# First FFN of a two-block kernel: x laid out by features as a second input, the norm's factor put on gate sums and residual, first units loaded by halves

## Chip, cores and metric

One core of a Trainium2 chip runs the whole program in one launch. The metric is the device time in microseconds of one execution; three executions of the kernel before took 1588.74, 1589.74 and 1584.87 us, median 1588.74.

## The reference, cut to what matters

A sequence of 256 tokens with 1024 features passes two blocks in fp32: FFN, attention mixer, FFN, norm; then, twice, FFN, mixer (RWKV, then stick-breaking attention), FFN with layer norms. The change concerns the very first sublayer:

```
def rmsnorm(x, g):
    xf = x.astype(jnp.float32)
    y = xf * lax.rsqrt(jnp.mean(xf * xf, axis=-1, keepdims=True) + RMS_EPS)
    return (y * g.astype(jnp.float32)).astype(x.dtype)

def swiglu(h, w_gate, w_up, w_down):
    return (jax.nn.silu(h @ w_gate) * (h @ w_up)) @ w_down

x = x + 0.5 * swiglu(rmsnorm(x, norm_ffn1[l]), w_ffn1_gate[l], w_ffn1_up[l], w_ffn1_down[l])
```

The FFN's hidden width is 2816, 22 tiles of 128. The factor 1/sqrt(mean) is one number per token, so it can be put on the products as well as on x.

## The kernel before

**Units.** All weights come as "units" of 128 x 2048 fp32 (1024 KB) in the order of use, from `ws`. The first FFN has 33 units: a gate unit holds one 128-column tile of the gate matrix (s = 0) and one of the up matrix (s = 1), a down unit holds two 128-row tiles of the down matrix. The order (`ffn_order`, L53) is gate 0, gate 1, then nine times (gate 2j+2, down j, gate 2j+3), then gate 20, gate 21, down 9, down 10. So unit 3 is the first "down".

**Split.** Each value is a sum of a high part (rounded to the format fp32r) and a low part (the rest). ScalarE writes the high part of a unit (`hi_to`, L200, instruction at L210), VectorE subtracts it for the low part (`lo_to`, L213, instruction at L224). There are three raw buffers, four high and three low ones. SP loads unit u (`load_units`, L186) once the low part of unit u-3 has been written, since then its raw buffer is free. A product is high x high, high x low and low x high. TensorE reads x as `xt`: features on the partitions, eight blocks of 128 features, two halves of the tokens, high and low.

**Beginning (L3128 to L3159).** SP loads x by two halves of tokens (512 KB each), the gain row broadcast to all partitions (512 KB), units 0 to 2, small vectors, constants. ScalarE squares x with a row sum (L348) and takes the root (L350), VectorE the mean and reciprocal, and multiplies x by the token's factor and by the gain row (L336). TensorE turns the result by sixteen transposes (L247), ScalarE and VectorE copy it from PSUM as high and low parts (L277, L284). Then TensorE multiplies units 0, 1 and 2: first high x (high, low) of the first tokens (`first_tensor`), then the rest (`second_tensor`). Their sums go into banks 0 to 5.

**FFN.** From unit 3 each engine has its own program. For unit n ScalarE (`ffn_scalar`, L693) first makes high parts up to unit n+3, waiting for its load, and only then treats gate n: it copies the cross products of the gate tile from PSUM (`lead_scalar`, L488, for the first three units; `wide_scalar`, L609, for the others), silu of the gate sum (L707, with a table load ahead of the first), the cross products of the up tile, and the high part of the hidden tile (L716). VectorE (`ffn_vector`, L724) first makes low parts up to unit n+2, then adds cross products and own products (L501 for the first three, L616 for the others) for s = 0 and s = 1, multiplies silu and up sum (L742) and subtracts the high part (L745). Each of these orders is fixed, and a wait holds whatever stands behind it.

TensorE (`ffn_tensor`, L644) waits for the low part of the unit. A gate unit takes eight matmuls of 512 columns and eight of 256 for each s. From unit 4 they go into three banks in turn (`gate_bank`, L574), and a bank is taken again when the event `s_tt` of the sum that read it has come:

```
    banks = (6, 4, 5) if t == "f1" else (6, 7, 4, 5)
    q = 2 * (f - 3) + s
```

So the up tile of gate f waits for the gate sum of gate f-1, and the gate tile of f for the up sum of f-2. The first down unit waits for the up sum of gate 1 as well.

**Beside it.** After gate 3 TensorE makes a small product of distances into bank 7 (`bias_tensor`, L1112). VectorE copies it, and POOL writes it out eight times, 512 KB each (`bias_pool`, L1139), the i-th behind the product of silu and up of gate 2+i; two large reads follow. These writes share the DMA engines with the units.

Of the kernel before, what the change touches and what calls it, by code (L numbers as in the profile page):

```python
# [8 lines left out]
F32 = mybir.dt.float32  # L9
# [105 lines left out]
def tiles_and_signals(nc, ctx, k):  # L115
# [5 lines left out]
    def sig(name):  # L121
# [187 lines left out]
class Rms:  # L309


    def __init__(self, k, t, scale, sums, ready, gain, free=None):

        self.k, self.t, self.scale, self.sums, self.ready, self.gain, self.free = k, t, scale, sums, ready, gain, free

    def add_vector(self, dve, a, h):
        k = self.k
        if self.sums is None:
            return
        dve.wait_ge(*self.sums(a, h))  # L320
        xs = k.x[:, a, h * 512:(h + 1) * 512]
        dve.e.scalar_tensor_tensor(out=xs, in0=k.P[2 * a + h][:, :], scalar=self.scale, in1=xs, op0=ALU.mult,
                                   op1=ALU.add).then_inc(*k.s_res.inc(self.t, a, h))

    def rest_vector(self, dve, a):
# [12 lines left out]

    def scalar(self, act, a):
        k, t = self.k, self.t  # L340
        if self.sums is None:
            act.wait_ge(*self.ready(a))
        else:
            for h in range(2):
                act.wait_ge(*k.s_res.after(t, a, h))
# [267 lines left out]
def wide_vector(k, dve, event, b, cross, out, scale=1.0):  # L613

    dve.wait_ge(*k.s_tb.after(*event))
    dve.e.scalar_tensor_tensor(out=out.rearrange("p (a t) -> p a t", a=2), in0=wide_parts(k, b)[0], scalar=scale,  # L616
                               in1=cross.rearrange("p (a t) -> p a t", a=2), op0=ALU.mult,
                               op1=ALU.add).then_inc(*k.s_tt.inc(*event))


def down_tensor(k, pe, u, j, i, a, hs=(0, 1)):
# [319 lines left out]
def mixer_tiles(k):  # L941
# [37 lines left out]
    k.MV = ar(k, 20480, 512, "p (a c) -> p a c", a=2)  # L979
    k.MEM = ar(k, 3072, 2048, "p (a n) -> p a n", a=2)  # L980
    k.JUNK = k.XN
    k.cross, k.mx_cross = crosses(k, 15360), crosses(k, 15856)


# [126 lines left out]

def bias_tensor(k, pe, j):  # L1112
    if j == 0:
        pe.wait_ge(*k.s_base.after())
        pe.wait_ge(*k.s_rel.after())
        mm(pe, k.P[7][0:16, :], k.RELX, k.BASE).then_inc(*k.s_pe.inc("dist"))
# [1926 lines left out]


def sync_program(k, sp):
    for a in range(2):
        sp.e.dma_start(k.x[:, a, :], k.x_in[a * 128:(a + 1) * 128, :]).then_inc(*k.s_x[a].inc(by=16))
    load_gains(k, sp, "f1", (0,))
    load_units(k, sp, 0, NRAW)
    sp.e.dma_start(k.vc[:, :], k.vec[:, :]).then_inc(*k.s_vec.inc(by=16))  # L3050
    sp.e.dma_start(k.cs[:, C_TRI:C_END], k.cst[:, C_TRI:C_END]).then_inc(*k.s_cst.inc(by=16))

    def gains(name, rows_, after):
        for w in after:
# [10 lines left out]
    gains("f2", (2,), normed("mx"))  # L3065
    load_units(k, sp, U_MIX + 10, U_FFN2 + 6)
    gains("f3", (3,), normed("f2"))
    load_units(k, sp, U_FFN2 + 6, U_FFN3 + 6)
    gains("rw", (4, 5), normed("f3"))
    load_units(k, sp, U_FFN3 + 6, U_RWKV + 15)  # L3070
    gains("f4", (6, 7), [k.s_pe.after("read", 1)])
# [3 lines left out]
    gains("f5", (8, 9), normed("f4"))  # L3075
    load_units(k, sp, U_FFN4 + 6, U_FFN5 + 6)
    gains("sb", (10, 11), normed("f5"))
    load_units(k, sp, U_FFN5 + 6, U_FFN6 + 1)
    gains("f6", (12, 13), [k.s_tr.after("sbmemo")])
    load_units(k, sp, U_FFN6 + 1, U_FFN6 + 6)  # L3080
    gains("end", (14, 15), normed("f6"))
    load_units(k, sp, U_FFN6 + 6, NU)
    for a in range(2):
        for h in range(2):
            sp.wait_ge(*k.s_xn.after("end", a, h))
        sp.e.dma_start(k.out[a * 128:(a + 1) * 128, :], k.x[:, a, :]).then_inc(*k.s_out.inc(a, by=16))
    sp.wait_ge(*k.s_out.after(1))


def pool_program(k, pool):  # L3090
    pool.e.dma_start(k.cs[:, 0:C_TRI], k.cst[:, 0:C_TRI]).then_inc(*k.s_id.inc(by=16))
    pool.e.dma_start(k.BASE, k.base[:, :]).then_inc(*k.s_base.inc(by=16))
    pool.e.dma_start(k.RELX, k.relx[:, :]).then_inc(*k.s_rel.inc(by=16))
    bias_pool(k, pool)
# [17 lines left out]
def norms(k):  # L3112

    k.norm = {
        "f1": Rms(k, "f1", 1.0, None, lambda a: k.s_x[a].after(), "f1"),
        "mx": Rms(k, "mx", 0.5, ffn_sums(k, "f1", U_FFN1), None, "mx", "f1"),
        "f2": Rms(k, "f2", 1.0, rows_done(k, "mx", U_MIX + 19), None, "f2", "mx"),
        "f3": Rms(k, "f3", 0.5, ffn_sums(k, "f2", U_FFN2), None, "f3", "f2"),
        "rw": LayerNorm(k, "rw", 0.5, ffn_sums(k, "f3", U_FFN3), "rw"),
        "f4": LayerNorm(k, "f4", 1.0, rows_done(k, "rw", U_RWKV + 14), "f4"),  # L3120
        "f5": LayerNorm(k, "f5", 0.5, ffn_sums(k, "f4", U_FFN4), "f5"),
        "sb": LayerNorm(k, "sb", 0.5, ffn_sums(k, "f5", U_FFN5), "sb"),
        "f6": LayerNorm(k, "f6", 1.0, rows_done(k, "sb", U_SB + 13), "f6"),
        "end": LayerNorm(k, "end", 0.5, ffn_sums(k, "f6", U_FFN6), "end"),
    }


def begin_tensor(k, pe):  # L3128

    turn_tensor(k, pe, "f1", tiles(k.XN), halves(k.s_xn, "f1"))  # L3130
    units = first_units(U_FFN1)
    for n in range(3):
        first_tensor(k, pe, "f1", units[n], n)
    for n in range(3):
        second_tensor(k, pe, "f1", units[n], n)


def begin_scalar(k, act):
    act.wait_ge(*k.s_dv.after("one"))
    act.e.activation(k.sm[:, 31:32], k.sm[:, 30:31], ACT.Sqrt)  # L3140
    for a in range(2):
        k.norm["f1"].scalar(act, a)
    turn_scalar(k, act, "f1", None, FIRST, (4, 5))
    hi_to(k, act, U_FFN1 + 1)
    turn_scalar(k, act, "f1", None, SECOND, (6, 7))
    hi_to(k, act, U_FFN1 + 3)


def begin_vector(k, dve):
    dve.e.memset(k.sm[:, 30:31], 1.0).then_inc(*k.s_dv.inc("one"))  # L3150
    for a in range(2):
        k.norm["f1"].rest_vector(dve, a)
    turn_vector(k, dve, "f1", FIRST, (4, 5))
    lo_to(k, dve, U_FFN1)
    turn_vector(k, dve, "f1", SECOND, (6, 7))
    lo_to(k, dve, U_FFN1 + 2)


# [91 lines left out]
    vector_program(k, Stream(engines[4], real))  # L3250


def build(nc, ws, cst, vec, base, relx, gains, x_in, mem_in, lora, gup, w2, out):
    k = Space()
    k.ws, k.cst, k.vec, k.base, k.relx, k.gains, k.x_in, k.mem_in = ws, cst, vec, base, relx, gains, x_in, mem_in
    k.lora, k.gup, k.w2, k.out = lora, gup, w2, out
    with ExitStack() as ctx:
        tiles_and_signals(nc, ctx, k)
# [54 lines left out]
def lay_out(i):  # L3313
# [79 lines left out]
    for l in range(2):  # L3393
        for n in range(3):
            g2 += [i["ln_g_2"][l, n], i["ln_b_2"][l, n]]
    gains = np.stack([i["norm_ffn1"][0], i["norm_mix"][0], i["norm_ffn2"][0], i["norm_final"]] + g2)
# [22 lines left out]
```

## Time and profile before

| what | value |
|---|---|
| median of three runs | 1588.74 us (1584.87 to 1589.74) |
| span of the profiled execution | 1585.7 us (the page gives no other time of it) |
| TensorE busy | 1553.6 us, 98% |
| VectorE busy | 1037.7 us, 65% |
| ScalarE busy | 864.8 us, 55% |
| DMA | 285.08 MB, mean 180 GB/s |

All times on a row of the trace are microseconds from the first instruction of the span, so they stand a little under the device time of a run. "Busy" of TensorE counts pipelined matmuls, whose ends are modelled: the difference of two starts says more than a duration. A timeline row that merges n instructions gives the start of the first and the time to the end of the last.

### The profile page before, as it was taken

How to read it: one execution, taken by the hardware profiler on the slowest of the kernel's cores; microseconds unless marked ns; L12 is line 12 of the kernel's file. 1: busy time of each engine (PE TensorE's matmuls, PEld its weight loads, DVE VectorE, ACT ScalarE, POOL GpSimd, SP SyncE). 2: the span in 40 equal slices, each digit the busy share in tenths (PEclk: the TensorE clock that was granted, in tenths of full speed). 3: DMA queues.
4: the chain of work that ended last, by engine and by line, in shares of the span. 5: the costliest groups of instructions: out<-in, count | busy, mean ns of one | idle time of the engine just before them, and what ended most of it. 6: DMA issues, size and time to landing. Idle time of an engine off the chain costs nothing. (4 is left out here: it accounts for less than half of the span.)

```text
span 1585.7 us, 26471 instructions
## 1 busy us (share of the span) xinstructions
PE 1553.6 (98%) x11174; PEld 1355.8 (86%) x11174; DVE 1037.7 (65%) x1477; ACT 864.8 (55%) x1270; POOL 131.2 (8%) x124
## 2 busy tenths in 40 slices
PE   7999999999999999999999999999999999999998
PEld 6888888688888988889988888889888888898886
DVE  6556676766566665667965775657756675676566
ACT  6455556655555555556753365555655565665553
POOL 0000020000000010002564001000100010001000
PEclk9999999999999999999999999999999999999999
DMA  7997546246555465555310365553655542455551
GB/s 289 236 263 266 199 160 249 81 175 217 205 186 186 159 216 209 176 194 181 128 48 4 134 231 194 186 196 137 251 194 179 190 181 80 160 211 188 201 175 75
DMA packets 42133, 285.08 MB, mean 180 GB/s; under 512 B 4906, under 2 KB 4922, under 8 KB 10144
## 3 DMA queue, kind: packets, MB, share of 16 engines
q1 hardware_dynamic: 39024, 272.42, 48.8%
q0 software_dynamic: 2992, 10.99, 3.3%
q8 instruction: 88, 1.44, 0.4%
q14 instruction: 29, 0.24, 0.0%
HBM read 277.62 MB, written 5.24 MB: 178 GB/s over the span
## 5 line engine op out<-in xcount | busy, mean ns | idle before, releaser
L236 PE MATMUL P<-xt,whi 128*128 128x512 f32 (+1 forms) x3264 | 723.6, 345 | 6.4 <-DVE AR L616 2.3
L236 PEld LDWEIGHTS P<-xt,whi 128*128 128x128 f32 x3264 | 557.3, 190 | 76.6 <-issue 7.3
L224 DVE TENSOR_TENSOR wlo<-raw,whi 128x2048 fp32r<-128x2048 f32 x245 | 559.5, 2290 | 55.6 <-PE P L236 47.4
L210 ACT ACTIVATE whi<-raw 128x2048 fp32r<-128x2048 f32 x245 | 467.7, 1910 | 149.5 <-PE P L236 83.9
L236 PE MATMUL P<-xt,wlo 128*128 128x256 f32 x2544 | 439.7, 282 | 0.0
L236 PEld LDWEIGHTS P<-xt,wlo 128*128 128x128 f32 x2544 | 386.8, 191 | 17.8
L616 DVE SCALAR_TENSOR_TENSOR AR<-P,AR 128x256 f32<-128x256 f32 x228 | 96.2, 422 | 244.4 <-ACT AR L609 244.3
L236 PE MATMUL P<-whi,hh 128*128 128x512 f32 x504 | 197.4, 392 | 0.0
L236 PE MATMUL P<-wlo,hh 128*128 128x512 f32 x504 | 196.8, 391 | 0.0
L236 PE MATMUL P<-whi,hl 128*128 128x512 f32 x504 | 196.1, 389 | 0.0
L609 ACT ACTIVATE AR<-P 128x256 f32<-128x256 f32 x228 | 85.5, 375 | 118.0 <-PE P L236 117.9
L236 PE MATMUL P<-whi,xt 128*128 128x512 f32 (+2 forms) x400 | 125.5, 376 | 0.4 <-DVE xt L2645 0.4
L716 ACT ACTIVATE hh<-AR 128x256 fp32r<-128x256 f32 x126 | 52.7, 418 | 112.6 <-DVE AR L742 112.6
L236 PEld LDWEIGHTS P<-whi,hl 128*128 128x128 f32 x504 | 94.6, 188 | 20.2
L236 PEld LDWEIGHTS P<-whi,hh 128*128 128x128 f32 x504 | 94.8, 188 | 18.0
L236 PEld LDWEIGHTS P<-wlo,hh 128*128 128x128 f32 x504 | 94.9, 188 | 17.3
L707 ACT ACTIVATE AR<-AR 128x256 f32<-128x256 f32 x132 | 55.1, 418 | 91.0 <-DVE AR L616 84.7
L236 PE MATMUL P<-AR 64*64 64x64 f32 (+8 forms) x2422 | 95.8, 244 | 2.1 <-issue 1.1
L745 DVE TENSOR_TENSOR hl<-AR,hh 128x256 fp32r<-128x256 f32 x126 | 55.6, 441 | 61.0 <-ACT hh L716 61.0
L236 PEld LDWEIGHTS P<-AR 64*64 64x64 f32 (+6 forms) x2422 | 74.3, 139 | 19.6 <-issue 8.9
L236 PEld LDWEIGHTS P<-whi,xt 128*128 128x128 f32 x400 | 72.8, 189 | 13.4 <-issue 1.0
L515 POOL TENSOR_SCALAR x<-x 128x1024 f32<-128x1024 f32 x10 | 32.8, 3297 | 571.2 <-DVE AR L742 414.0
(228 smaller groups left out, 1012.6 us busy)
## 6 DMA issues: line engine op xcount, KB each, us to landing
raw<-ws SPq DMA_DIRECT2D x249, 1024.0 KB, 4.9
gb<-gains SPq DMA_DIRECT2D x14, 512.0 KB, 7.3
by_distance<-AR POOLq DMA_DIRECT2D x8, 512.0 KB, 8.3
AR<-by_distance POOLq DMA_DIRECT2D x1, 2048.0 KB, 17.1
AR<-by_distance POOLq DMA_DIRECT2D x1, 1536.0 KB, 9.1
x<-x_in SPq DMA_DIRECT2D x2, 512.0 KB, 3.8
AR<-mem_in POOLq DMA_DIRECT2D x1, 1024.0 KB, 5.2
AR<-gains SPq DMA_DIRECT2D x2, 512.0 KB, 4.6
```

Of the source, the lines that this page charges most:

```text
L210: act.e.activation(k.whi[n % NHI][:, :], k.raw[u % NRAW][:, :], ACT.Copy).then_inc(*k.s_hi.inc(u))
L224: dve.e.tensor_tensor(k.wlo[n % NLO][:, :], k.raw[u % NRAW][:, :], k.whi[n % NHI][:, :].bitcast(F32), ALU.subtract).then_inc(*k.s_lo.inc(u))
L236: return pe.e.matmul(o, l, r, start=start, stop=stop, skip_group_check=True)
L515: pool.e.tensor_scalar(k.x[:, a, :], k.x[:, a, :], ALPHA / scale, None, ALU.mult).then_inc(*k.s_al.inc(t, a))
L609: act.e.activation(cross.rearrange("p (a t) -> p a t", a=2), wide_parts(k, b)[1], ACT.Copy, scale=scale).then_inc(*k.s_tb.inc(*event))
L616: dve.e.scalar_tensor_tensor(out=out.rearrange("p (a t) -> p a t", a=2), in0=wide_parts(k, b)[0], scalar=scale, in1=cross.rearrange("p (a ...
L707: act.e.activation(k.SL[:, f % 2, :], k.cross[f % 3][:, 0, :], ACT.Silu).then_inc(*k.s_sl.inc(t, f))
L716: act.e.activation(hh, k.HF[:, f % 2, :].rearrange("p (a t) -> p a t", a=2), ACT.Copy).then_inc(*k.s_hh.inc(t, f))
L745: dve.e.tensor_tensor(hl, k.HF[:, f % 2, :].rearrange("p (a t) -> p a t", a=2), hh.bitcast(F32), ALU.subtract).then_inc(*k.s_hl.inc(t, f))
```

## The change

x comes a second time, laid out by features (`x_col`, 128 x 2056, made beside the other inputs): eight columns with the norm weights of the first FFN, then eight blocks of 128 features by 256 tokens. `xt` is made from it directly: ScalarE copies a block times its column of norm weights (high part), VectorE multiplies again and subtracts (low part). There is no turn. Units 0 and 1 are loaded, and their parts made, by halves (s = 0, s = 1), the first half's high part by quarters. TensorE takes all three units as it takes later ones: 512 columns of high by (high, low), then 256 of low by high, and waits per feature block at the beginning.

x by tokens is loaded behind and is still squared with a row sum; root and reciprocal give the token's factor. Two diagonal matrices with these factors, multiplied from the left by ones, put the factors as a row on all partitions (bank 7), and ScalarE copies it as `RROW`. VectorE multiplies every gate sum of the first FFN by `RROW` (22 times 128x256, ahead of silu), and the event for which ScalarE and the next user of the bank wait, `s_tt`, moves behind that multiplication. The up sums are not multiplied. The factor for them, times 0.5, is put on the residual (the scale of that addition is a column of factors instead of the constant 0.5). The gain rows lose their first row, and the mixer's gain row is loaded without a wait.

The core of the diff (changes of signatures and row numbers left out):

```diff
@@ lead_vector
-                                   op1=ALU.add).then_inc(*k.s_tt.inc(t, n, s))
+                                   op1=ALU.add).then_inc(*summed(k, t, n, s))
+        if rooted(t, s):
+            rooted_vector(k, dve, t, n, out[:, s, :])
+
+def rooted(t, s):
+    return t == "f1" and s == 0
+
+def summed(k, t, f, s):
+    return k.s_dv.inc("gate sum", f) if rooted(t, s) else k.s_tt.inc(t, f, s)
+
+def rooted_vector(k, dve, t, f, part):
+    dve.wait_ge(*k.s_ea.after("rrow"))
+    dve.wait_ge(*k.s_dv.after("gate sum", f))
+    dve.e.tensor_tensor(part, part, k.RROW, ALU.mult).then_inc(*k.s_tt.inc(t, f, 0))
@@ wide_vector: the same for the other gates
@@ sync_program
-    for a in range(2):
+    def tokens(a):
         sp.e.dma_start(k.x[:, a, :], k.x_in[a * 128:(a + 1) * 128, :]).then_inc(*k.s_x[a].inc(by=16))
-    load_gains(k, sp, "f1", (0,))
-    load_units(k, sp, 0, NRAW)
+    def part(u, s):
+        w = slice(1024 * s, 1024 * s + 1024)
+        sp.e.dma_start(k.raw[u][:, w], k.ws[u, :, w]).then_inc(*k.s_part[u][s].inc(by=16))
+    sp.e.dma_start(k.XCOL[:, 0:1032], k.x_col[:, 0:1032]).then_inc(*k.s_col[0].inc(by=16))
+    part(0, 0)
+    sp.e.dma_start(k.XCOL[:, 1032:2056], k.x_col[:, 1032:2056]).then_inc(*k.s_col[1].inc(by=16))
+    part(0, 1)
+    tokens(0)
+    part(1, 0)
+    tokens(1)
+    part(1, 1)
+    load_units(k, sp, 2, NRAW)
...
-    gains("mx", (1,), normed("f1"))
+    gains("mx", (0,), [])
@@ pool_program
+    pool.e.memset(k.ONE, 1.0).then_inc(*k.s_po.inc("one"))
@@ norms
-        "mx": Rms(k, "mx", 0.5, ffn_sums(k, "f1", U_FFN1), None, "mx", "f1"),
+        "mx": Rms(k, "mx", lambda a: k.sm[:, 12 + a:13 + a], ffn_sums(k, "f1", U_FFN1), "mx"),
+def begin_high_tensor(k, pe, u, s):
+    wh, _ = weights(k, u)
+    for c in range(8):
+        pe.wait_ge(*k.s_xl.after("f1", c))
+        if u == 2:
+            pe.wait_ge(*k.s_hi.after(u))
+        else:
+            pe.wait_ge(*k.s_hi.after("part", u, s, 1 if u or s else c // 4))
+        w = slice((s * 8 + c) * 128, (s * 8 + c) * 128 + 128)
+        mm(pe, k.P[LEAD_BANKS[u][s]][:, :], wh[:, w], k.xt[:, c, :, :, :].rearrange("p a s t -> p (a s t)"), c == 0, False)
@@ begin_tensor
+    for u in range(3):
+        for s in range(2):
+            begin_high_tensor(k, pe, u, s)
+        if u == 1:
+            pe.wait_ge(*k.s_po.after("one"))
+            for a in range(2):
+                pe.wait_ge(*k.s_dv.after("diag", a))
+                last = mm(pe, k.P[7][:, 128 * a:128 * a + 128], k.ONE, k.DIAG[:, a, :])
+            last.then_inc(*k.s_pe.inc("rrow"))
+        for s in range(2):
+            last = begin_low_tensor(k, pe, u, s)
+        last.then_inc(*k.s_used.inc(u))
@@ begin_scalar
+    for c in range(4):
+        high(c)
+    part(0, 0, 0, 1)
+    for c in range(4, 8):
+        high(c)
+    part(0, 0, 1, 2)
+    part(0, 1, 0, 2)
+    square(0)
+    part(1, 0, 0, 2)
+    square(1)
+    part(1, 1, 0, 2)
+    act.wait_ge(*k.s_var.after("f1"))
+    act.e.activation(k.sm[:, 6:8], k.sm[:, 10:12], ACT.Sqrt).then_inc(*k.s_rt.inc("f1"))
+    hi_to(k, act, U_FFN1 + 2)
+    act.wait_ge(*k.s_pe.after("rrow"))
+    act.e.activation(k.RROW, k.P[7][:, 0:256], ACT.Copy).then_inc(*k.s_ea.inc("rrow"))
     hi_to(k, act, U_FFN1 + 3)
```

VectorE's beginning follows the same order: eight low parts of x, low(0, 0), low(0, 1), low(1, 0), the mean, low(1, 1), the reciprocal, two diagonals (128x128), the half factor, the low part of unit 2.

## Rows read from the trace of the kernel before

**Rows 1.** The page's busy times by engine: us, share of the span, instructions.
```profile
PE 1553.6 (98%) x11174; PEld 1355.8 (86%) x11174; DVE 1037.7 (65%) x1477; ACT 864.8 (55%) x1270; POOL 131.2 (8%) x124
```

**Rows 2.** TensorE's waits, whole run: us in total, times, longest.
```profile
PE P L236 <- DVE AR L616: 2.3, 2, 1.2
```

**Rows 3.** TensorE's timeline, 8 to 116 us: start, us, instruction, [idle before <- releaser].
```profile
8.86 3.82 PE L247 MATMUL P<-cs,AR 128*128 128x128 f32 x16 [8.86 <-DVE AR L336]
13.28 4.10 PE L236 MATMUL P<-xt,whi 128*128 128x256 f32 x32 [0.61 <-ACT whi L210]
...
31.39 0.40 PE L236 MATMUL P<-whi,hh 128*128 128x512 f32 x1
...
36.86 1.98 PE L236 MATMUL P<-xt,whi 128*128 128x512 f32 x8
...
64.18 2.11 PE L236 MATMUL P<-xt,whi 128*128 128x512 f32 x8 [1.05 <-DVE AR L616]
...
82.29 2.11 PE L236 MATMUL P<-xt,whi 128*128 128x512 f32 x8 [1.23 <-DVE AR L616]
...
99.01 2.00 PE L236 MATMUL P<-xt,whi 128*128 128x512 f32 x8
```

**Rows 4.** ScalarE's timeline, 20 to 25 us.
```profile
20.58 1.92 ACT L210 ACTIVATE whi<-raw 128x2048 fp32r<-128x2048 f32 x1 [2.78 <-DMA raw<-ws]
23.91 0.66 ACT L493 ACTIVATE AR<-P 128x256 f32<-128x256 f32 x2 [1.41 <-PE P L236]
24.58 1.28 ACT L707 ACT_TABLE_LOAD   x1
```

**Rows 5.** VectorE's timeline, 7 to 30 us.
```profile
7.96 1.42 DVE L336 SCALAR_TENSOR_TENSOR AR<-x,sm,gb 128x512 f32<-128x512 f32 x2 [2.03 <-DMA gb<-gains]
...
27.65 2.28 DVE L224 TENSOR_TENSOR wlo<-raw,whi 128x2048 fp32r<-128x2048 f32 x1
29.85 0.74 DVE L501 SCALAR_TENSOR_TENSOR AR<-P,AR 128x256 f32<-128x256 f32 x2
```

**Rows 6.** SP's timeline, then DMA issues: times, KB each, us to landing.
```profile
0.73 0.84 SPq L3047 DMA_DIRECT2D x<-x_in  x2
4.13 0.44 SPq L3051 DMA_DIRECT2D cs<-cst  x1
...
x<-x_in SPq DMA_DIRECT2D x1, 512.0 KB, 3.4
x<-x_in SPq DMA_DIRECT2D x1, 512.0 KB, 4.2
cs<-cst SPq DMA_DIRECT2D x1, 752.0 KB, 13.3
raw<-ws SPq DMA_DIRECT2D x1, 1024.0 KB, 4.9
raw<-ws SPq DMA_DIRECT2D x1, 1024.0 KB, 13.8
```

**Rows 7.** Transposes: weight loads near 9 us, products near 200 us.
```profile
8.83 1.57 PEld L247 LDWEIGHTS P<-cs,AR 128*128 128x128 f32 x8 [8.83 <-issue]
...
200.00 0.60 PE L247 MATMUL P<-cs,AR 128*128 128x128 f32 x4
```

**Rows 8.** Stretches: us, PE, (PEld, DVE, ACT, POOL) busy, PEclk, DMA share, GB/s.
```profile
9.00:11.00 2.00, 2.00 (x10) 1.00 1.01 422
...
80.00:120.00 40.00, 38.77 (x208) 33.41 (x207) 23.81 (x27) 20.83 (x28) 2.87 (x4) 1.00 0.92 266
```

**Rows 9.** Waits for the raw buffers' loads, 0 to 140 us: us, times.
```profile
  DMA raw<-ws: 32.4, 10
```

**Rows 10.** ScalarE's timeline near 61 us.
```profile
61.49 1.92 ACT L210 ACTIVATE whi<-raw 128x2048 fp32r<-128x2048 f32 x1 [8.57 <-DMA raw<-ws]
```

**Rows 11.** VectorE's timeline: gate sums near 63 and 98 us.
```profile
63.70 0.42 DVE L616 SCALAR_TENSOR_TENSOR AR<-P,AR 128x256 f32<-128x256 f32 x1 [6.53 <-ACT AR L609]
...
98.37 0.42 DVE L616 SCALAR_TENSOR_TENSOR AR<-P,AR 128x256 f32<-128x256 f32 x1 [4.09 <-ACT AR L609]
```

More of the change, by code:

```diff
@@ L145, in tiles_and_signals @@
     k.s_gn = [sig("gn0"), sig("gn1")]
+    k.s_col = [sig("col0"), sig("col1")]
+    k.s_part = [[sig(f"part{u}{s}") for s in range(2)] for u in range(2)]
     k.s_id, k.s_vec, k.s_cst, k.s_base, k.s_rel = (
@@ L340, in scalar @@
         k, t = self.k, self.t
[L341 to L345, printed above, removed]
+        for h in range(2):
+            act.wait_ge(*k.s_res.after(t, a, h))
         if self.free is not None:
@@ L617, in wide_vector @@
                                in1=cross.rearrange("p (a t) -> p a t", a=2), op0=ALU.mult,
-                               op1=ALU.add).then_inc(*k.s_tt.inc(*event))
+                               op1=ALU.add).then_inc(*summed(k, *event))
+    if rooted(event[0], event[2]):
+        rooted_vector(k, dve, event[0], event[1], out)
 def down_tensor(k, pe, u, j, i, a, hs=(0, 1)):
@@ L1113, in bias_tensor @@
     if j == 0:
+        pe.wait_ge(*k.s_ea.after("rrow"))
         pe.wait_ge(*k.s_base.after())
@@ L3125, in norms, with begin_low_tensor @@
     }
-def begin_tensor(k, pe):
[L3130 to L3135, printed above, removed]
+def begin_high_tensor(k, pe, u, s):
[8 more added lines that the diff above has]
+        mm(pe, k.P[LEAD_BANKS[u][s]][:, :], wh[:, w], k.xt[:, c, :, :, :].rearrange("p a s t -> p (a s t)"), c == 0, False)
+def begin_low_tensor(k, pe, u, s):
+    _, wl = weights(k, u)
+    own, _ = lead_parts(k, u, s)
+    pe.wait_ge(*(k.s_lo.after(u) if u == 2 or s else k.s_lo.after("part", u)))
+    for c in range(8):
+        w = slice((s * 8 + c) * 128, (s * 8 + c) * 128 + 128)
+        last = mm(pe, own, wl[:, w], k.xt[:, c, :, 0, :], False, c == 7)
+    return last
+def begin_tensor(k, pe):
+    for u in range(3):
[10 more added lines that the diff above has]
+        last.then_inc(*k.s_used.inc(u))
 def begin_scalar(k, act):
@@ L3150, in begin_vector, with low @@
     dve.e.memset(k.sm[:, 30:31], 1.0).then_inc(*k.s_dv.inc("one"))
-    for a in range(2):
[L3152 to L3155, printed above, removed]
+    def low(u, s):
+        w = slice(1024 * s, 1024 * s + 1024)
+        dve.wait_ge(*k.s_hi.after("part", u, s, 1))
+        dve.e.tensor_tensor(k.wlo[u][:, w], k.raw[u][:, w], k.whi[u][:, w].bitcast(F32),
+                            ALU.subtract).then_inc(*(k.s_lo.inc(u) if s else k.s_lo.inc("part", u)))
+    for c in range(8):
+        dve.wait_ge(*k.s_xh.after("f1", c))
+        dve.e.scalar_tensor_tensor(out=k.xt[:, c, :, 1, :], in0=k.XRAW[:, c, :, :], scalar=k.GCOL[:, c:c + 1],
+                                   in1=k.xt[:, c, :, 0, :].bitcast(F32), op0=ALU.mult,
+                                   op1=ALU.subtract).then_inc(*k.s_xl.inc("f1", c))
+    low(0, 0)
+    low(0, 1)
+    low(1, 0)
+    for a in range(2):
+        dve.wait_ge(*k.s_sq.after("f1", a))
+    dve.e.tensor_scalar(k.sm[:, 10:12], k.sm[:, 4:6], 1.0 / DM, 1e-6, ALU.mult, ALU.add).then_inc(*k.s_var.inc("f1"))
+    low(1, 1)
+    dve.wait_ge(*k.s_rt.after("f1"))
+    dve.e.reciprocal(k.sm[:, 10:12], k.sm[:, 6:8]).then_inc(*k.s_dv.inc("f1", "rstd"))
+    dve.wait_ge(*k.s_id.after())
+    dve.wait_ge(*k.s_dv.after("f1", "rstd"))
+    for a in range(2):
+        dve.e.tensor_scalar(k.DIAG[:, a, :], k.cs[:, C_ID:C_ID + 128], k.sm[:, 10 + a:11 + a], None,
+                            ALU.mult).then_inc(*k.s_dv.inc("diag", a))
+    dve.e.tensor_scalar(k.sm[:, 12:14], k.sm[:, 10:12], 0.5, None, ALU.mult).then_inc(*k.s_dv.inc("f1", "half"))
+    dve.lo = U_FFN1 + 2
     lo_to(k, dve, U_FFN1 + 2)
@@ L3402, in lay_out @@
         "ws": ws, "cst": cst, "vec": vec, "base": base, "relx": relx, "gains": gains, "x_in": i["x"][0],
+        "x_col": np.concatenate([cols_of(i["norm_ffn1"][0]), by_cols(i["x"][0].T, slice(0, NT))], axis=1),
         "mem_in": i["mem_2"][0], "lora": lora, "gup": i["rwkv_g_up_2"][0],
```

57 lines of the change are left out of this document (33 added, 24 removed).

## Prediction

> **What bounds the kernel now.** I read the page's busy times first: TensorE is busy 98% of the span, VectorE 65%, so time can come only from TensorE's gaps or its work [rows 1]. Then TensorE's waits: in the whole run it waits twice for a gate sum, 2.3 us together [rows 2]. Its timeline shows both in the first FFN (they end at 64.18 and 82.29), and the beginning: nothing until the transposes at 8.86, the first matmul at 13.28, and from 17.86 no gap until the first "down" product at 31.39 [rows 3]. The change can take at most what lies ahead of 31.39. The timelines of ScalarE and VectorE tell who would hold TensorE if it came earlier, and the DMA issues when the data is there.
>
> **Until the first three units are multiplied.** What goes: the norm of x (square, root, reciprocal, product with the gain row, whose load VectorE awaits until 7.96), sixteen transposes (3.82 us) and their copies. What comes, for each of eight feature blocks: one ScalarE copy and one VectorE operation of 128x256. A pair of such copies takes ScalarE 0.66 us, so 0.33 each in a row; VectorE's pair takes 0.74 [rows 4, 5]. Loads land in the order of issue. The first 512 KB land at 0.73+3.4 = 4.1, the second, issued about 0.42 later, at 5.35 (4.2 behind it): 1.25 us per 512 KB. The gain row behind them took until 7.96, so 2.6 [rows 5, 6]. The new order (columns, half unit, columns, half unit, tokens, half, tokens, half, unit 2, vectors, constants) has two loads of 512 KB more, the columns, and lacks the slow gain row: two at 1.25 for one at 2.6. So the queue empties as before, at 4.13+13.3 = 17.4.
>
> Step by step: first columns 4.1; four copies to 5.5; first half unit 5.4. Second columns between 6.6 (by 1.25) and 7.96 (the gain row's place); I take 7.3, since POOL's small constants pass then too. Four copies to 8.6; the second quarter of unit 0's high part (a whole one takes 1.92, so 0.55 with its overhead) to 9.2; the next half (1.0) to 10.2. TensorE starts in earnest at 9.2 and is paced to 10.2. Then come 40 matmuls of 512 columns and 48 of 256. Eight of the first take 1.98 with a tail of 0.4, so 0.227 apart; 32 of the second 4.10, so 0.12 apart [rows 3]: 9.1+5.8, and 0.5 for the two products that make the row of factors, 15.4 in all. TensorE is through with three units at 25.6, not 31.39: 5.8 us earlier. Squares (1024 elements at ScalarE's rate: 1.0 each), root, reciprocal and two diagonals lie between, on engines that wait for loads, and TensorE has six blocks of work before it needs the factors.
>
> One cost is hidden here. The removed transposes ran 0.21 us apart (eight weight loads in 1.57 with a tail), the same operation at 200 us 0.11 (four in 0.60 with a tail of 0.27), though the granted clock is printed 1.00 from 9 to 11 us [rows 7, 8]. If the first sixteen wide matmuls run at half the rate instead, TensorE is through at 25.6+16x0.2 = 28.8. The Trainium skill, "TensorE: Matmul & The Clock Gate", section "What's actually happening", says that throttled is the default and that activity releases it. By it the transposes paid for the matmuls behind them, and the change hands the bill to the matmuls. The spacing agrees, the clock column doesn't; the next step makes either end harmless.
>
> **The first "down" product, where the gain is cut.** ScalarE's order has the high part of unit 3 ahead of the sums of unit 0. In the trace it waits 2.78 us for its load, starts at 20.58, and ScalarE still waits 1.41 for TensorE afterwards [rows 4]. Now TensorE is early and the load is last. Unit 3 is issued once unit 0's buffer is free, near 11, behind a queue that empties at 17.4; with 2.5 for its 1024 KB it lands at 20.0 (bounds: 19.0, and 25.4 if each half of a unit goes as the gain row did, four times 1.35 more). From there I copy the trace's own spacing. Sums begin 1.83 after that high part, 21.85. The low part of unit 3 begins 3.74 after them (27.65-23.91) and ends at 27.9; the second gate's sum begins 5.94 after them (29.85-23.91), at 27.8 [rows 4, 5]. Behind it stands the new multiplication, 0.42 long, starting 0.46 after the sum as such pairs do; then the up sum, so that the event for which the first down product waits comes at 27.8+0.85+0.42 = 29.05. For the first gate the multiplication costs nothing, the table load of 1.28 covers it. TensorE, through at 25.6 to 28.8, starts "down" at 29.05, not 31.39: **2.35 us** gained, whatever the early part does. The rest becomes a wait there.
>
> **The rest of the first FFN.** All 22 gates pay the multiplication, about 10 us of VectorE, which is idle for a third of the time. Where TensorE sets the pace it is hidden: the up sum waits for the up product anyway. Where a load sets the pace it isn't. Between 80 and 120 us the DMA engines are at 92% [rows 8]: the by-distance writes, each started behind a gate's product, share with the units, and a unit that lands 4.9 after issue when alone takes 13.8 [rows 6]. ScalarE waits 32.4 us for units in ten waits up to 140 us, 8.57 in the longest, which ends at 61.49 [rows 9, 10]. Behind it the gate's sum is late, at 63.70, and TensorE waits for its event at 64.18; the same happens at 82.29, and a third time the sum ends at 98.79 where TensorE starts the bank that needs it at 99.01, with 0.22 to spare [rows 3, 11].
>
> Now the triggers of writes and loads all move: the chain of ScalarE and VectorE behind "down" is 1.6 to 2.1 earlier (2.35 less the multiplications not hidden), so the load of 61.49 lands about 1.8 earlier. Its gate's event is then 1.8-0.45 = 1.35 earlier, while TensorE, 2.35 ahead, stalls a us more and leaves at -1.35. The next unit is issued behind the same gate's chain, so each such round can add 0.45: -0.9 at 82.29; at 98.79 the event is at -0.45 and TensorE waits there too; about -0.4 if every landing passes its delay on. If the queue is full anyway, landings go by bytes and not by issue, and -1.35 stays. I take between them: **-0.9 us**. Once the writes are done a unit takes 4.9 again, and the shift stays.
>
> **Other edits.** The residual's factor from a column instead of a constant, the missing wait for the turn, the changed gain rows: the same instructions in the same places, 0 (bounds -0.2 to +0.2). The mixer's gain row loses its wait and stays between the same units: 0. POOL's fill of ones stands ahead of two constant loads that nobody needs before 42 us: 0. SP issues three more loads at 0.42 each [rows 6], in the shadow of a full queue: 0.
>
> **Against the clock.** The span of 1585.7 becomes 1584.8. The page gives no time of the profiled execution but its span; the median 1588.74 is 3.0 above it. Forecast 1588.74-0.9 = **1587.8 us**.
>
> **Rivals.**
> B, the pattern of loads moves as a whole and the multiplications hide in it: -2.35, 1586.4. For it: every write is triggered by a gate's product and moves along. Against: the 0.22 us to spare at 99.01.
> C, the whole early gain stays: -5.8, 1582.9. It needs unit 3 landed by about 17, while the queue was full until 17.4.
> D, slower, by the half loads: pieces of 4 KB a row go as the gain row did, 2.6 instead of 1.25 per 512 KB. Unit 3 lands at 25.4, "down" starts at 34.4, +3.0, and the multiplication at the stalls adds 0.45 to 0.9: about 1592. It decides from a landing of unit 3 behind 22.4. For it: the gain row is a 512 KB load too. Against: the loads of x, with rows of the same size, are 1.25 apart. The Trainium skill, "DMA: Bandwidth & Descriptors", section "Anatomy of one DMA", gives each DMA a fixed 2.0 us beside its bytes; paid in line that would be, an estimate by that page, +2.0 for each added transfer, and speaks for D. The 1.25 between the loads of x speaks against it: the fixed part overlaps.
> E, the multiplication adds up at all seven load-paced gates (ten waits, less two before 40 us and one behind 125): 7x0.45 = 3.15 against 2.35, +0.8, 1589.5.
>
> **Chances.** Forecast 0.50, B 0.22, C 0.06, D 0.09, E 0.13. A difference of 0.3%, 4.8 us, is about what a measurement can tell from none: forecast, B and E are inside it, C outside, D half outside, and medians scatter (single runs go from 1584.87 to 1589.74). Faster 0.10, same 0.84, slower 0.06. Range 1584.2 to 1590.8: from B less 2 us of scatter to E and 1.3 more.
>
> **What would show it.** In the changed kernel: the first wide matmul near 6, no gap between 10.2 and 25 (28.8 at half rate), a wait of up to 3.5 us ahead of the first "down" product, ended by VectorE near 29; ScalarE's wait for unit 3 until 20; then stalls before gates longer than 1.05 and 1.23, possibly a third near 98. I am wrong if unit 3 lands before 18 or behind 22.4, if "down" starts more than 1 us from 29, if the shift at 120 us is outside -2.4 to +0.8, or if stages behind 200 us change, which no edit touches.

## The result, and the profile after

The changed kernel takes 1590.88 us (median of 13 runs, 1588.58 to 1593.23), the kernel before 1587.70 in as many: **3.2 us slower, ratio 1.0022, 95% interval 1.0014 to 1.0030**. The forecast was 1587.8, which is 0.9 below the 1588.74 that the kernel before had by then, and a difference too small to tell from none; the range ended at 1590.8. The profiled execution has a span of 1589.2, 3.5 us more than that of before.

The page's busy times: TensorE has no more work than before (1553.6) [rows 1], VectorE 10.3 us more, of which the 22 multiplications (0.425 each) are 9.4.

```profile
PE 1553.4 (98%) x11114; PEld 1352.9 (85%) x11114; DVE 1048.0 (66%) x1502; ACT 866.3 (55%) x1277; POOL 131.0 (8%) x125
```

So the loss is in TensorE's gaps, and in stretches that it spends at the lower clock. TensorE's timeline (start, us, instruction, [idle before <- releaser]) against [rows 3]:

```profile
7.12 2.04 PE L238 MATMUL P<-xt,whi 128*128 128x512 f32 x4 [7.12 <-DVE xt L3253]
10.09 4.33 PE L238 MATMUL P<-xt,whi 128*128 128x512 f32 x12 [0.93 <-DVE xt L3253]
...
25.88 2.07 PE L238 MATMUL P<-xt,wlo 128*128 128x256 f32 x16
30.51 0.77 PE L238 MATMUL P<-whi,hh 128*128 128x512 f32 x1 [2.56 <-issue]
...
65.28 2.11 PE L238 MATMUL P<-xt,whi 128*128 128x512 f32 x8 [1.54 <-DVE AR L519]
...
82.63 2.11 PE L238 MATMUL P<-xt,whi 128*128 128x512 f32 x8 [0.48 <-DVE AR L519]
...
116.97 2.12 PE L238 MATMUL P<-xt,whi 128*128 128x512 f32 x8 [0.56 <-DVE AR L519]
```

TensorE is through with three units at 27.95, waits 2.56 us, and starts "down" at 30.51 instead of 31.39: 0.9 us gained of 3.4. The stalls now end on L519, the new multiplication. At 65.28 the kernel stands 1.1 us behind before, at 116.97 1.35 (115.62 there).

ScalarE's and VectorE's timelines show what TensorE waits for at 30.51, as in [rows 4, 5]: unit 3 lands at 21.46 (20.0 in the prediction), and the chain behind it has the forecast spacings, to the multiplication and the up sum that ends at 30.4.

```profile
21.46 1.92 ACT L212 ACTIVATE whi<-raw 128x2048 fp32r<-128x2048 f32 x1 [0.56 <-DMA raw<-ws]
23.28 0.64 ACT L490 ACTIVATE AR<-P 128x256 f32<-128x256 f32 x2
```
```profile
27.00 2.28 DVE L226 TENSOR_TENSOR wlo<-raw,whi 128x2048 fp32r<-128x2048 f32 x1
29.21 0.41 DVE L498 SCALAR_TENSOR_TENSOR AR<-P,AR 128x256 f32<-128x256 f32 x1
29.65 0.42 DVE L519 TENSOR_TENSOR AR<-AR 128x256 f32<-128x256 f32 x1
30.00 0.41 DVE L498 SCALAR_TENSOR_TENSOR AR<-P,AR 128x256 f32<-128x256 f32 x1
```

What I had not seen coming stands in the stretches around 30 us (us, TensorE busy, granted clock, DMA share, GB/s): from 30.0 on, still inside the wait, the clock is granted at 0.50, the 1.2 GHz level. I call such a stretch a half clock.

```profile
27.90:30.50 2.60, 0.05 (x1) 0.91 0.49 118
30.50:31.50 1.00, 0.99 (x2) 0.50 0.42 139
31.50:32.50 1.00, 1.00 (x4) 0.50 1.08 451
32.50:33.50 1.00, 1.00 (x4) 0.53 0.83 352
33.50:34.50 1.00, 1.00 (x6) 1.00 0.02 8
```

The first down unit takes from 30.51 to the next unit's first matmul,

```profile
37.45 1.98 PE L238 MATMUL P<-xt,whi 128*128 128x512 f32 x8
```

6.94 us, against 36.86-31.39 = 5.47 before [rows 3]. So 1.47 us are lost there, more than the 0.9 gained, and the gate unit behind starts 0.6 late.

Then there is a place that the change doesn't touch, in the last FFN:

```profile
1415.78 0.47 PE L238 MATMUL P<-whi,hh 128*128 128x512 f32 x1 [0.62 <-issue]
```

In the trace of before nothing stands there.

**Where the 3.5 us of the two spans are.** I took VectorE's low part of each unit (the same operation in both kernels, matched from the end) and the difference of its two starts. Each column is named by the time of that start in before; 0 is as early as in the first trace of before, +1.5 is 1.5 us later. The column 210 stands behind the first FFN. TensorE's own position is the same there to 0.1 us, and in every trace it doesn't move between 122 and 210 us.

| kernel | 210 | 299 | 403 | 748 | 881 | 1404 | 1443 | half clock at |
|---|---|---|---|---|---|---|---|---|
| before | 0 | 0 | 0 | 0 | 0 | 0 | 0 | 306 |
| before, repeated | +0.4 | -0.5 | -0.5 | -0.8 | +0.8 | +0.7 | +0.8 | 304, 758 |
| changed | +1.5 | +1.9 | +0.4 | +0.1 | +3.0 | +2.6 | +3.5 | 30 |
| changed, repeated | +1.6 | +0.3 | -0.9 | -1.2 | +1.8 | +1.7 | +2.8 | 32, 759 |
| fill | +1.6 | +1.6 | +1.8 | +2.0 | +3.0 | +2.7 | +2.6 | 66 |
| mult_only | +3.2 | +2.0 | +1.9 | +1.6 | +3.3 | +2.9 | +2.9 | 68, 307, 761 |
| early | +2.1 | +2.8 | +1.4 | +1.0 | +3.2 | +2.9 | +3.9 | 64, 760 |
| nomult | -1.2 | -0.9 | -0.5 | -0.5 | +0.3 | 0.0 | +1.0 | 305, 759 |
| before_spread | -2.1 | -2.2 | -2.0 | -2.3 | -1.1 | -1.3 | -1.3 | 303, 757 |
| mult_only_spread | -2.5 | -3.6 | -3.4 | -3.3 | -1.5 | -1.8 | -1.7 | 302, 756 |
| changed, spread (after_spr) | -1.6 | -1.1 | -2.3 | -2.7 | -0.6 | -0.9 | +0.3 | 32, 756 |
| early_free_spread | -5.7 | -5.1 | -5.1 | -5.3 | -1.4 | -1.7 | -0.8 | 300, 754 |
| the same, repeated (efs_rep) | -5.4 | -5.5 | -7.0 | -6.5 | -2.0 | -2.2 | -1.2 | 751 |

"Half clock at" lists where the granted clock is 0.50 (for 3.4 us each, 6.8 in early near 64 and in the last line; the end of the program left out). Single traces scatter. The two of before differ by 0.8 at the end, since half clocks near 305 and 758 come in most executions and not in all. They differ by 1.4 at 28 us already, of which 1.1 comes between 13 and 19: in the second one products of 256 columns start 0.21 us apart until 17.7, in the first 0.12 from 13.3 on. The first FFN costs the changed kernel 1.1 to 1.6 us against the two. Of the rest 0.9 to 1.2 comes between 1404 and 1443, and 2.5 (repeated: 1.3) between 780 and 881, behind the place of the half clock. Between 299 and 403 it gets 1.4 (repeated: 1.2) back, for neither of its traces has the half clock near 305.

### The profile page after: what moved, and what is told of

The parts are those of the page before. It is cut to its first block and busy times, and to the rows that moved or that the text cites. A ratio compares the mean times of both kernels' runs of the same rounds, so it can differ in the third digit from the quotient of the medians.

```text
span 1589.2 us, 26386 instructions
## 1 busy us (share of the span) xinstructions
PE 1553.4 (98%) x11114; PEld 1352.9 (85%) x11114; DVE 1048.0 (66%) x1502; ACT 866.3 (55%) x1277; POOL 131.0 (8%) x125
## 5 line engine op out<-in xcount | busy, mean ns | idle before, releaser
L238 PE MATMUL P<-xt,wlo 128*128 128x256 f32 x2544 | 434.6, 283 | 0.0
L632 DVE SCALAR_TENSOR_TENSOR AR<-P,AR 128x256 f32<-128x256 f32 x228 | 96.3, 422 | 235.5 <-ACT AR L625 235.3
L238 PEld LDWEIGHTS P<-wlo,hh 128*128 128x128 f32 x504 | 95.3, 189 | 17.4
L238 PEld LDWEIGHTS P<-AR 64*64 64x64 f32 (+4 forms) x2426 | 75.1, 139 | 21.4 <-issue 10.9
## 6 DMA issues: line engine op xcount, KB each, us to landing
AR<-by_distance POOLq DMA_DIRECT2D x1, 2048.0 KB, 15.4
```

The source lines that it names most:

```text
L238: return pe.e.matmul(o, l, r, start=start, stop=stop, skip_group_check=True)
```

## Experiments

Two theories went in. **Load pace**: the multiplications lengthen the way from a landed unit to the next issue, in the stretch where the by-distance writes make unit loads late; TensorE's stall grows there and gives back what the beginning gains. **Clock**: the new wait ahead of "down" costs by the half clock behind it. A third question was whether the gaps far behind belong to the kernel.

**again**, the changed kernel with no edit.

> The changed kernel itself once more, for what repeats. Theory clock: the wait ahead of the first down product returns (about 2.6 us, TensorE through with unit 2 near 28) and behind it TensorE's granted clock is 0.50 for some 3.4 us, so the first down unit takes about 1.5 us more than the 5.47 of before. Theory chance: the half clock is an accident of the one profiled execution and is absent here. For the rest of the program: if the gaps named issue in the RWKV stage (820 to 880 us, 2.4 us more than before) and at 1412 us (0.6 more) belong to the kernel, they return in size and place; if they belong to the execution, they don't. Time against before: +3 us (+0.2%).

1591.12 us, ratio 1.0025 (1.0011 to 1.0038). The wait (1.89 us, "down" at 30.51) is there again, the half clock too (here from 31.6), and so is the gap of 0.92 us at 1415. The stall at 66.39 is 2.44. What repeats, then: the half clock near 30 and the gap near 1415. The 2.5 us in the RWKV stage, between 780 and 881, become 1.3.

**fill**, with eleven products ahead of the wait, whose results are never read.

```diff
+        if t == "f1" and n == 3:
+            for c in range(11):
+                mm(pe, k.P[6][:, :], k.xt[:, 0, 0, 0, :], k.xt[:, c % 8, :, :, :].rearrange("p a s t -> p (a s t)"))
         pe.wait_ge(*k.s_lo.after(u))
```

> Eleven matmuls of 512 columns into an unused bank, their results never read, stand in TensorE's order ahead of the wait for unit 3, so that TensorE works while it would wait (11 x 0.227 = 2.5 us). Theory clock: granted clock 1.00 throughout 30 to 34 us, the first down unit takes 5.5 us instead of 6.94, and everything behind is up to 1.5 us earlier at 50 us; of it about 1 us is kept, the kernel is 1 us faster than the changed one. Theory multiplication (the loss is all from the 22 multiplications of gate sums at load-paced gates): the position at 116 us and the time don't change.

1590.01 us, ratio 1.0017 (1.0008 to 1.0026). The clock stays at 1.00, as forecast:

```profile
30.00:31.00 1.00, 1.00 (x7) 1.00 0.65 98
31.00:32.00 1.00, 1.00 (x6) 1.00 0.55 180
```

But the stall at the load-paced gate swallows it, and the clock falls at that one instead (from 65.6 on):

```profile
65.82 3.58 PE L238 MATMUL P<-xt,whi 128*128 128x512 f32 x8 [2.89 <-DVE AR L519]
```
```profile
66.00:67.00 1.00, 1.00 (x3) 0.50 0.93 393
```

At 210 us it stands where the changed kernel stands, +1.6. That the half clock near 30 comes of the gap is shown, and that its absence there gains nothing. But a half clock of the same length stands at the next stall instead, and TensorE's position moves by 1.5 us under it (from +1.6 at 64 to +3.1 at 68), as it did by 1.47 near 30. What a kernel with neither would gain, fill doesn't show.

**mult_only**, the kernel before with the multiplications alone.

```diff
+        if rooted(t, s):
+            rooted_vector(k, dve, t, n, out[:, s, :])
...
+    pool.e.memset(k.RROW, 1.0).then_inc(*k.s_po.inc("ones"))
```

> The kernel before with only the 22 multiplications of gate sums by a row (of ones, so that nothing is changed in value), with the event behind them. Nothing of the beginning is touched. Theory multiplication: TensorE's stalls of 1.05 and 1.23 in the first FFN grow by 0.45 each and a third and a fourth appear near 99 and 115 us, together +1 to +2 us at 120 us. Theory clock: only about +0.9 (the two stalls) in position and no half clock near 30 us; the time differs from before by under 1 us.

1589.97 us, **ratio 1.0017 (1.0008 to 1.0025)**: 2.5 us of the 3.2 without anything of the new beginning. ScalarE gets the unit of 61.49 [rows 10] at 64.15, and in place of 1.05 us TensorE stalls 3.79:

```profile
64.15 1.91 ACT L210 ACTIVATE whi<-raw 128x2048 fp32r<-128x2048 f32 x1 [10.81 <-DMA raw<-ws]
```
```profile
67.30 3.18 PE L236 MATMUL P<-xt,whi 128*128 128x512 f32 x8 [3.79 <-DVE AR L519]
```
```profile
68.50:69.50 1.00, 1.00 (x4) 0.50 0.28 107
```

The load took 15.4 us from issue to landing (13.8 in [rows 6]). At 210 us the kernel is 3.2 late, more than both forecasts. TensorE's position (at times of before) shows where: +0.4 at 60, +3.1 at 64.2, +4.7 at 68 behind the half clock, +3.2 at 84 (where before has its second stall), and no change after that. From the landed unit to TensorE's start it takes 3.15 us for 2.69 in before, which is the multiplication, once. The half clock is 1.6. The rest is the late landing, and single traces don't settle how much of that is the multiplication's: before, repeated, gets the same unit at 63.31, and its load took 14.3 us.

**early**: ScalarE's and VectorE's order around the first two gates. ScalarE's part:

```diff
     hi_to(k, act, U_FFN1 + 2)
+    act.e.activation(k.sm[:, 31:32], k.sm[:, 30:31], ACT.Silu)
     act.wait_ge(*k.s_pe.after("rrow"))
     act.e.activation(k.RROW, k.P[7][:, 0:256], ACT.Copy).then_inc(*k.s_ea.inc("rrow"))
-    hi_to(k, act, U_FFN1 + 3)
...
+    for f in range(2):
+        lead_scalar(k, act, t, U + f, f, k.cross[f])
+    silu(0)
+    hi_to(k, act, U + 3)
+    silu(1)
```

> The changed kernel with ScalarE's and VectorE's order around the first two gates changed: sums of gates 0 and 1 and the first silu ahead of unit 3's high part, table of silu loaded in an idle stretch. The chain sets the first down product at 29 to 30.5 in the changed kernel; here the low part of unit 3 ends near 27.7 and the hidden tile's at 28, so TensorE waits under 0.5 us, the first down product starts near 28.1, and the clock stays 1.00: the first down unit is done 4 us earlier than in the changed kernel. Theory of a DMA-paced middle: most of that comes back as longer stalls at 64 and 82 us, of the 4 us some 1.5 to 2 stay. Theory of a plain shift: all 4 us stay and the kernel beats before by about 1 us.

1590.38 us, ratio 1.0024 (1.0011 to 1.0038). The wait ahead of "down" is gone, its start is 0.95 earlier than in the changed kernel, and the clock stays up. Nothing of it is left at 65:

```profile
29.56 0.47 PE L238 MATMUL P<-whi,hh 128*128 128x512 f32 x1 [0.15 <-DVE hl L736]
...
65.53 3.78 PE L238 MATMUL P<-xt,whi 128*128 128x512 f32 x8 [4.16 <-DVE AR L519]
```

The stall is 4.16 instead of 1.54, with 6.8 us at half clock from 63.7 on. The forecast that 1.5 to 2 us stay is missed. The unit of 61.49 is there at 62.38. TensorE was 1.8 us ahead of before at 60, but the load was issued at 47.84 for 47.64: TensorE came earlier, the load didn't.

**nomult**, with `rooted` false everywhere: it leaves the token's factor out of silu's argument.

```diff
-    return t == "f1" and s == 0
+    return False
```

> The changed kernel without its 22 multiplications of gate sums (the factor per token is left out of silu's argument); the new beginning stays whole. Theory multiplication (the 22 multiplications delay the chain from a landed unit to the next load, which paces TensorE from 45 to 120 us): position against before at 154 us falls from +1.5 to about -0.5, the stall near 65 us is under 2 us, and the time is that of before or 1 us less (ratio 0.9995 to 1.0003). Rival, the beginning itself costs (the wait of 2.6 us ahead of the first down product and the half clock behind it): position and time stay at +1.5 and 1.001 or more.

In position it is further ahead than expected: -1.2 at 210 us for -0.5 (at 154 us it is the same). So the two parts add up there: the multiplications cost 2.7 in the new kernel (+1.5 against -1.2) and 2.8 to 3.2 in the old one, and the beginning gains 1.2 to 1.7 in either. No half clock comes with its waits, and of the 2.7 the half clock near 30 is 1.5.

```profile
30.33 0.47 PE L238 MATMUL P<-whi,hh 128*128 128x512 f32 x1 [1.43 <-DVE wlo L226]
...
64.52 2.11 PE L238 MATMUL P<-xt,whi 128*128 128x512 f32 x8 [2.37 <-DVE AR L632]
```

The stall at 64.52, on the plain sum L632, was to be under 2. In time it is a miss: ratio 1.0016 (1.0001 to 1.0031), when 1.0003 was the most. Two of its twelve executions (1597.49 and 1597.89 us) make more than half of that. The medians are 1588.11 and 1586.94, ratio 1.0007, and 1.0 us stands between 1404 and 1443.

**before_spread, mult_only_spread, early_free_spread**: the test at the root, with the writes spread over time.

```diff
-            pool.wait_ge(*k.s_hf.after("f1", 2 + i))
+            pool.wait_ge(*k.s_hf.after("f1", (3, 4, 6, 7, 9, 10, 12, 13)[i]))
```

and in early_free_spread, beside early's order, the bank given back at the sum and no longer behind the multiplication:

```diff
+                if added is not None and rooted(t, added[2]):
+                    pe.wait_ge(*k.s_dv.after("gate sum", added[1]))
```

> The kernel before with the by-distance writes issued behind the products of gates 3, 4, 6, 7, 9, 10, 12, 13 instead of 3 (twice), 4, 5 to 9. Theory load pace: the unit that lands at 61.49 lands about 5 us earlier, the two stalls of 1.05 and 1.23 us go, and the kernel is 2 us faster than before (ratio 0.9985). Rival: the DMA engines are full in the mean anyway and the stalls move behind 90 us; no difference.

> Both: the 22 multiplications alone, and the writes spread. Theory: a multiplication costs nothing where TensorE sets the pace, so this is as fast as before_spread (within 0.6 us) and its TensorE has no stall over 1 us in the first FFN. Rival: the multiplications cost by themselves (VectorE's order, late hidden tiles), and it is 2.5 us slower than before_spread, as mult_only is slower than before.

> The changed kernel with the order of the first two gates changed as in early, banks given back at the gate sum instead of behind the multiplication, and the writes spread. Theory load pace: what the new beginning gives at the first down product (29.56 against 31.39, 1.8 us) now stays, and the stalls go: 1.8 us faster than before_spread, 3.5 us faster than before (ratio 0.998). Rival: the chain of ScalarE and VectorE up to unit 7 holds the pace, and it equals before_spread.

| kernel | median us | ratio to before |
|---|---|---|
| before_spread | 1585.68 | 0.9992 (0.9983 to 1.0000) |
| mult_only_spread | 1585.15 | 0.9989 (0.9980 to 0.9998) |
| early_free_spread | 1583.39 | **0.9979 (0.9971 to 0.9988)** |

The unit comes earlier, at 58.41 (before_spread) and 56.76 (early_free_spread). before_spread was to get it 5 us earlier and to be 2 us faster: it got 3.1 and 1.3, with an interval that reaches 1.0000. The other two came as forecast, early_free_spread 2.3 us faster than before_spread for 1.8.

```profile
58.41 1.92 ACT L210 ACTIVATE whi<-raw 128x2048 fp32r<-128x2048 f32 x1 [4.80 <-DMA raw<-ws]
```
```profile
56.76 1.92 ACT L212 ACTIVATE whi<-raw 128x2048 fp32r<-128x2048 f32 x1 [5.36 <-DMA raw<-ws]
```

All of TensorE's waits up to 200 us in mult_only_spread are those of the beginning; the stalls on sums are gone:

```profile
PE P L247 <- DVE AR L336: 9.1, 1, 9.1
PE P L236 <- ACT whi L210: 1.4, 2, 0.9
```

The multiplications cost 2.5 us with the writes as they were and nothing (-0.5) with the writes spread. That decides: they have no price of their own, they have one where a load sets the pace. With the pace lifted, the order changed and the bank given back earlier, the new beginning is worth something: at 210 us early_free_spread is 5.7 us ahead of before, 3.2 more than mult_only_spread, and in time 1.8 us faster than that. Order and bank weren't tried apart. Its two traces, of executions 2.8 and 1.5 us slower than the medians of their sets, lose 2.3 and 1.8 us between 780 and 881.

**before_rep, after_spr, warmbest.** before_rep is the kernel before, after_spr the changed one with the spread writes alone, warmbest is

```diff
+    pe.wait_ge(*k.s_po.after("one"))
+    for c in range(10):
+        mm(pe, k.P[7][:, 0:128], k.ONE, k.ONE)
```

> The kernel before once more, for what repeats in its trace. If the half clock near 759 us, which nearly all runs of kernels with and without the change show and the first trace of before doesn't, comes with the execution and not with the kernel, it may be present here; the first trace of before is then 1.5 us short there. The gap named issue of 0.6 to 0.9 us near 1412 us appears in every kernel with the new beginning but in none with the old: it must be absent. TensorE's stalls at 64 and 82 us as before, 1 to 1.3 us. Time: that of before, ratio 1.000.

> The changed kernel with nothing but the by-distance writes spread. Theory load pace: the changed kernel's loss of 3.5 us against before came from the load-paced stretch, so here it is gone: as fast as mult_only_spread or up to 0.9 us faster, less the half clock behind the first down product (1.5) and the issue gap near 1412 us (1.0): ratio to before 0.9990 to 1.0000. Rival, the beginning costs by itself: 1.0015 or more.

> early_free_spread with ten small products of ones by ones into bank 7 (written over later) ahead of the first matmul, where TensorE idles until 7 us. Theory: the first twelve wide matmuls run at half rate in all kernels with the new beginning (12 in 4.3 to 5.5 us for 2.7); here they run at the full one, TensorE has the row of factors ready 1.5 us earlier, the first down product starts near 28 for 29.56, and the kernel is 1 to 1.5 us faster than early_free_spread (ratio 0.997). It also shifts TensorE's instruction stream by twenty, as fill did by eleven, where the issue gap near 1412 us was absent: it may go too, 1 us more. Rival: the copy of low parts and loads hold the pace, no difference.

before_rep: ratio 1.0004 (0.9994 to 1.0014), stall 1.48 at 66.00, half clock near 758 present, no gap at 1415; the first trace of before was a short one. after_spr: 1586.36 us, ratio 1.0003 (0.9989 to 1.0017), within reach of the forecast; no stall on a sum is left, the half clock behind "down" and the gap at 1415 (here at 1412.57) are. warmbest: 1587.37 us, ratio 1.0002 (0.9993 to 1.0011), a miss. The first four wide matmuls do run at full rate (1.16 us for 2.04), but behind the next gap the rate is half again, the granted clock is 0.50, and twelve take 4.49:

```profile
7.07 1.16 PE L238 MATMUL P<-xt,whi 128*128 128x512 f32 x4 [0.16 <-DVE xt L3303]
10.41 4.49 PE L238 MATMUL P<-xt,whi 128*128 128x512 f32 x12 [2.19 <-DVE xt L3303]
```
```profile
10.30:13.50 3.20, 3.09 (x7) 0.50 1.03 411
```

It stands like early_free_spread up to 299 us (-5.2) and ends 1.5 us behind it, by losses at other places: 1.2 between 346 and 403, 1.3 between 1295 and 1305.

**shift60, best_shift, efs_rep.** The first two put thirty tiny products, sixty instructions of TensorE, in front, in the changed kernel and in early_free_spread; efs_rep repeats early_free_spread.

```diff
+    for c in range(30):
+        mm(pe, k.P[7][:, 0:8], k.ONE, k.ONE[:, 0:8])
```

> The changed kernel with thirty tiny products of ones (8 columns, sixty instructions of TensorE) in the idle time before its first matmul, so that from the first down product on TensorE's stream stands at the place that it has in the kernel before (the change took sixty out). Theory stream: the gap named issue near 1415 us and the 1.0 us between 1404 and 1443 us go, as they are absent in every kernel with the old beginning and in fill; the kernel is 1 us faster than the changed one. Rival, it belongs to the execution: it is there in every execution of the new beginning, this one too. The loss in the load-paced stretch stays either way (+1.3 us at 154 us).

> early_free_spread with the sixty tiny instructions of shift60. Theory stream: as early_free_spread, less 1.0 us near 1412 us: ratio to before 0.997. Rival: the gap moves elsewhere in the program (the warmbest run had 1.3 us between 1297 and 1370 in its place), no difference to early_free_spread.

> early_free_spread once more, since warmbest, which differs only in ten small products at the start, was not faster than before. If early_free_spread's gain is real its ratio is again 0.997 to 0.999; if it was scatter between sets of runs, 1.000.

The sixty instructions took longer than I thought:

```profile
2.27 12.97 PE L238 MATMUL P<-AR 128*128 128x8 f32 x60 [2.27 <-POOL AR L3126]
```

so both kernels begin 5 us late and their times (1594.41, 1.0044; 1587.50, 1.0000) say nothing of the gap. Their traces do: between 1404 and 1443 the difference changes by -0.01 in both, as in fill, when it is +0.9 to +1.2 in all seven others with the new beginning but warmbest; and TensorE has no gap there. efs_rep: 1584.27 us, ratio 0.9988 (0.9976 to 1.0001), with the gap:

```profile
1411.09 0.47 PE L238 MATMUL P<-whi,hh 128*128 128x512 f32 x1 [0.75 <-issue]
```

So the gap hangs on how many instructions stand in TensorE's stream: all seven traces with 11114 have it, none of the nine with 11125 (fill), 11134 (warmbest) or 11174. warmbest suggests that another place can have one. What fills it is not shown. The two sets of early_free_spread are 3.6 and 2.9 us below before: the best version, with both medians below before's and one interval of two clear of 1.

## Why the prediction was wrong

**The early part** held in shape: first matmul 7.12 ("near 6"), steady from 10.09 (9.2 to 10.2), through at 27.95 (25.6 to 28.8, the half-rate end: twelve wide matmuls in 4.33). Putting this end aside as harmless was right.

**The first "down" product** held in its chain and not in the landing that starts it: unit 3 landed at 21.46, not 20.0, all else followed at the copied spacings, and "down" came at 30.51 for 29.05. The gain there was 0.9 for 2.35. The term that was off is "1.25 us per 512 KB": the first landed at 4.73 for 4.1, the next seven 1.40 apart, so the constants at 18.97 for 17.4; the last step, 2.5 to unit 3, was right. Rival D had the sign: unit 3 was 1.5 us late, where D had 5.4, since it charged a half unit what the gain row took. The 2.0 us for each DMA that the prediction takes for D from the Trainium skill, "DMA: Bandwidth & Descriptors", section "Anatomy of one DMA", are given there for DMAs issued from GpSimd, and these loads are SP's. The 1.40 shows that no such part was paid in line.

**What stood nowhere**: the wait that I forecast, "a wait of up to 3.5 us", has a price behind it. I weighed the clock for the beginning and not for the gap that I was making. It cost 1.47 us, so that TensorE stood at +0.6 from 37 to 60 us, where the forecast had -2.35. fill shows that it is the gap's doing, and that without it the next stall took its place.

**The step that failed** is "The rest of the first FFN", and in it "I take between them: -0.9 us", for a measured +1.5 behind 117. Its chain was the right one: load, high part, sum, multiplication, event. It started from the wrong place, as just said, and its premise "the load of 61.49 lands about 1.8 earlier" failed: the unit came at 62.12 (repeated: 63.24) for 61.49 (63.31), issued at 48.22 for 47.64. From 60 to 118 us TensorE lost another 0.9, where "each such round can add 0.45" and the stall of "a us more" had 1.45. So the multiplication's length was charged well enough, and what the longer waits set off was charged nothing: without the multiplications the kernel stands 2.7 us earlier, and 1.5 of that is the half clock.

Rival E, "the multiplication adds up", with 0.13, came closest, in part by luck. It had 3.15 us for the multiplications, measured 2.7 to 3.2, and 2.35 for the beginning, measured 1.2 to 1.7. Its path, 0.45 at each of seven gates, isn't what the traces show: in mult_only the length is paid at one, and a late landing and a half clock make up the rest. The lower end of the range, 1584.2, is 0.2 off its own working (1586.4 less 2).

**"If stages behind 200 us change, which no edit touches"**: they did. The change takes sixty instructions out of TensorE's stream, and 1.0 us turned up at 1415. The first profile of before was a short one as well, without the half clock near 758 that most executions have. The 1.3 to 2.5 us between 780 and 881, partly gaps named issue too (from 740 to 925: 2.3 us in four, in before 1.1 in two), go from 2.5 down to -0.4 over the kernels with the new beginning; I can't assign them.

Together: 1.1 to 1.6 us from the first FFN (multiplications +2.7, beginning -1.4), 1.0 near 1415, and about 1 that stays open, for 3.2 measured. What is open is the difference of two pieces of the traces: 1.3 to 2.5 lost behind 780, and 1.2 to 1.4 got back near 305.

## What to carry to other kernels

Work taken off the start is worth only what the next paced stretch lets through: look for the first long wait for a load behind it, and ask whether that load's trigger moves. An operation added to the chain from a landed buffer to the next issue can cost more than its length where loads set the pace, here 2.5 us where its length at two stalls would say 0.9, and nothing once the competing transfers are spread. Before shortening the work ahead of a wait, price the wait's other side: the clock after it.

## What the runs showed of the hardware

- A gap of TensorE can cost more than its length: with 1.89 to 2.56 us of waiting near 30 us came 3.4 us at a granted 0.50 in three traces (changed, repeated, after_spr), which cost 1.5 to 1.6 us; with 1.89 us in shift60, at 35.67, and 1.43 in nomult none came. With the later stalls of 1.05 to 2.84 us no half clock shows; with those of 2.89, 3.79 and 4.16 it does.
- A granted clock printed 1.00 doesn't vouch for the beginning: twelve matmuls of 512 columns took 4.33 to 5.46 us at 10 us and would take 2.9 at 0.227 apart plus the tail. The trace of the changed kernel has its first record of the clock, a 1.00, at 12.96 us; ahead of it the matmuls start 0.43 us apart, behind it 0.23. The Trainium skill, "TensorE: Matmul & The Clock Gate", section "What's actually happening", says that throttled is the default; the spacing agrees, and warmbest shows that ten products ahead lift it only up to the next gap.
- Thirty products of eight columns ran as sixty instructions with a fresh 128x128 weight each and took 12.97 us in the beginning (shift60), 0.216 each, as much as the transposes with 128 columns near 9 us (0.21): between 8 and 128 columns made no difference there.
- TensorE can have a gap that no wait in the trace explains, 0.62 to 0.93 us near 1415 us, and that goes when 11, 20 or 60 instructions are added to its stream 1400 us earlier.
